# A gated attention mixer at the end of a transformer kernel: second-branch products beside the last heads, gating by pairs, key scores released unit by unit

## The chip, the cores and the metric

The kernel is one program on one core of a Trainium2 chip. The metric is the time of one execution on the device in microseconds (us); the profile adds a span (first to last instruction) and the times of each engine: PE is TensorE, DVE is VectorE, ACT is ScalarE, POOL is GpSimd, SP is the engine that only issues DMAs here.

## The reference, cut to what matters

Two residual blocks of a small model (256 tokens, width 1024) run one after the other. Each of the first block's two layers ends in an expert layer that scores keys; the second block is a mixer with two branches and then an MLP:

```python
# expert layer, twice
q = (h @ wq).reshape(B, S, PEER_HEADS, 2, half)            # 16 groups of 128
s1 = einsum('bshd,hnd->bshn', q[..., 0, :], keys[:, 0])    # key scores
s2 = einsum('bshd,hnd->bshn', q[..., 1, :], keys[:, 1])
...                                                        # top 16, gates, experts u and v

# last mixer
q, k, v, su, sv, g_a, g_b = split(h @ w_in)
y_att = sliding_window_attention(q, k, v, ...)             # 8 heads, sinks, ALiBi
y_sgu = chunked_spatial_gating(su, sv, ...)                # products over tokens, times gelu(su)
merged = sigmoid(g_a) * (y_att @ w_oa) + sigmoid(g_b) * (y_sgu @ w_ob)
x = x + merged @ w_out
x = x + conv_gated_mlp(rmsnorm(x), ...)
```

## The kernel before

All weights stream through a ring of three slots (`RING`) as pieces of 128x1024 fp32 (512 KB each). SP starts the DMA of a piece into a slot (line 312) once the low part of the piece three before it has been made. A piece is split in two fp32r parts: ACT copies it to `w_hi` (line 508), then POOL (line 404) or DVE (line 1036) subtracts to make `w_lo`. PE then takes three products for each 128 rows: high by high, high weight by low activation, low weight by high activation. A piece marked `WHOLE` is not split: PE reads the ring slot itself in fp32. Every engine has its own instruction stream in program order, and semaphores tie them together; the order inside each stream is written out by hand.

The last mixer runs so. Its projections come first: queries and keys, values, the two halves of the spatial gating, then eight gate units (`one_unit(features)`, two pieces or 48 matmuls each; PE lines 1895, 1899, 1907), which ACT copies out of three rotating banks into `s_gate` (line 588). PE runs gate unit 0, then the 16 matmuls of the spatial gating (line 2458, `sgu_mixed`), then the scores of heads 0 to 2 (line 2319), then for each head: one gate unit (the filler), the transposes of the probabilities (line 2334), the scores of head h+3, the product with the values (lines 2342 and 2343). DVE makes the normed keys (line 1628), `s_vn` for the spatial gating (line 1694), the gating's sum and product `s_yb` (lines 1698 and 1704), and per head the masked scores (lines 1638 to 1645) and the scaled probabilities (lines 1650 to 1656). ACT exponentiates (lines 809 to 811) and copies the turned probabilities out (line 823).

After head 7, ACT and DVE split both branches' outputs into high and low parts (lines 522 and 1025). The eight pieces of `sb_ab` hold w_oa above w_ob, one output chunk of 128 columns each, so PE runs 24 matmuls for each chunk (lines 2475 to 2477) and DVE merges it: a product of the bank with both sigmoids (line 1715), an addition of its two halves (line 1717). The merged activations are split again and PE starts `add_to_stream` with w_out (line 1895, 1897, 1905 for its first piece).

In an expert layer, PE runs eight query units and then waits in line 2248 until all eight are out of their banks (DVE line 1107) before the key scores (line 2255), in eight groups of four matmuls.

Of the kernel before, what the change touches and what calls it, by code (L numbers as in the profile page):

```python
# [18 lines left out]
P = 128  # L19
T = 256  # L20
# [44 lines left out]
def build(nc, a, out):  # L65

    ctx = ExitStack()
    with ctx:
# [66 lines left out]
        def b3(ap, n):  # L135
# [125 lines left out]
                ("sb_in_c", "sb_in", 24, POOL), ("sb_ab", "sb_ab", 8, POOL), ("sb_out", "sb_out", 8, POOL),  # L261
                ("up", "up", 4, (POOL, DVE)), ("up_b", "up", 2 * FC - 4, DVE), ("down", "down", FC, DVE)]
        starts, maker = {}, []
        for name, _, count, who in RUNS:
            starts[name] = len(maker)
            maker += [who[j % 2] if isinstance(who, tuple) else who for j in range(count)]
# [41 lines left out]
        def _(sp):  # L308
# [5 lines left out]
            def stream(name, array, count):  # L314
                k0, at = starts[name], 0

                def piece(j):
                    if array == "ev_in":
                        return a[array][EV_ORDER[j]]
                    if array == "ev_out":  # L320
                        half, pair = 1 - j // 4, 2 * (j % 4)
                        return a[array][pair:pair + 2, :, half * 512:(half + 1) * 512].rearrange("o p n -> p o n")
# [14 lines left out]
                loops = (count - done) // BODY if not array.startswith("ev_") else 0  # L337
# [156 lines left out]
        def _(act):  # L494
# [85 lines left out]
            def unit(outs, func=ACT.Copy, pieces=2, scale=1.0, view=None):  # L580
# [4 lines left out]
                src = unit_bank(u[0])[:, 0:pieces * T]  # L585
# [218 lines left out]
            def attention(p, filler):  # L804
# [10 lines left out]
                for h in range(p["heads"]):  # L815
# [8 lines left out]
                    if h % 2:  # L824
                        act.wait_ge(g["at_mixed"], c + 1)
                        A(p["y"][:, h // 2, :], bank[7][:, 0:T], ACT.Copy).then_inc(g["at_y"], 1)

# [88 lines left out]
            act.wait_ge(g["units_out"], u[0])  # L916
            for c in range(KC):
                v = s_gate.rearrange("p (b c t) -> p b c t", b=2, c=KC)[:, :, c, :]
                A(v, v, ACT.Sigmoid).then_inc(g["gate_open"], 1)
# [87 lines left out]
        def _(dve):  # L1007
# [622 lines left out]
            def attention(p):  # L1630
                for h in range(p["heads"] + 1):
                    if h < p["heads"]:
# [12 lines left out]
                        V.tensor_scalar(sm[:, 0:2], sm[:, 0:2], nsink[:, h:h + 1], None, ALU.min).then_inc(g["at_masked"], 1)  # L1645
                    if h >= 1:
# [9 lines left out]
                        V.tensor_scalar(PR[:, P:3 * P], PR[:, P:3 * P], sm[:, 7:8], None, ALU.mult).then_inc(g["at_prob"], 1)  # L1656

# [38 lines left out]
            dve.wait_ge(g["sgu_mixed"], 1)  # L1696
            for j in range(2):
                step(V.tensor_tensor(s_mix[:, j * 512:(j + 1) * 512].rearrange("p (c b t) -> p c b t", c=2, b=TB),
                                     bank[6 + j][:, :].rearrange("p (c b t) -> p c b t", c=2, b=TB),
                                     s_bs[:, j * 256:(j + 1) * 256].rearrange("p (c o t) -> p c o t", c=2, o=1).to_broadcast([P, 2, TB, P]),  # L1700
                                     ALU.add))
            settle()
            dve.wait_ge(g["units_out"], u[0] + 8)
            V.tensor_tensor(s_yb, s_mix, s_u, ALU.mult).then_inc(g["sgu_y"], 1)
            attention(swa_att)
            u[0] += 16
            lows_of(big[:, at_y:at_y + 8 * T])
            dve.wait_ge(g["units_out"], u[0])
            n[0] += 31
            gates = s_gate.rearrange("p (b c t) -> p b c t", b=2, c=KC)  # L1710
            for c in range(KC):
                dve.wait_ge(g["pieces_used"], n[0] + c + 1)
                dve.wait_ge(g["gate_open"], c + 1)
# [885 lines left out]
```

## Time and profile before

| | us |
|---|---|
| median of 3 runs | 2280.3 (2279.82 to 2280.7) |
| profiled execution | 2284.43 |
| its span | 2281.5 |
| PE busy | 2234.4 (98%) |
| DVE busy | 1568.1 (69%) |
| ACT busy | 1189.8 (52%) |
| POOL busy | 774.2 (34%) |
| mean granted TensorE clock | 0.995 |

A busy PE is not a PE at its peak, since matmuls overlap. What the table says is that PE stands still for some 47 us out of 2281, in many places. The last mixer lies between about 1925 and 2081 us from the start of the span, the key scores at 202 and 1153 us.

### The profile page before, as it was taken

How to read it: one execution, taken by the hardware profiler on the slowest of the kernel's cores; microseconds unless marked ns; L12 is line 12 of the kernel's file. 1: busy time of each engine (PE TensorE's matmuls, PEld its weight loads, DVE VectorE, ACT ScalarE, POOL GpSimd, SP SyncE). 2: the span in 40 equal slices, each digit the busy share in tenths (PEclk: the TensorE clock that was granted, in tenths of full speed). 3: DMA queues.
4: the chain of work that ended last, by engine and by line, in shares of the span. 5: the costliest groups of instructions: out<-in, count | busy, mean ns of one | idle time of the engine just before them, and what ended most of it. 6: DMA issues, size and time to landing. Idle time of an engine off the chain costs nothing.

```text
span 2281.5 us, 43893 instructions
## 1 busy us (share of the span) xinstructions
PE 2234.4 (98%) x14296; PEld 1939.1 (85%) x14296; DVE 1568.1 (69%) x3187; ACT 1189.8 (52%) x1888; POOL 774.2 (34%) x766
## 2 busy tenths in 40 slices
PE   8999999999999999998999999999999999999999
PEld 7889888888888888897988888888888888888877
DVE  6733885888888755545258768888886555535885
ACT  4145555555444455565455565554444556556764
POOL 0027888222332000033778862223320002664000
PEclk9999999999999999998999999999999999999999
DMA  5345655555555566552555655555556655444655
GB/s 159 102 128 157 188 190 175 178 173 170 172 174 173 177 193 194 181 183 88 163 157 188 186 183 167 173 165 176 174 175 185 193 193 176 135 135 152 189 175 165
DMA packets 109649, 385.62 MB, mean 169 GB/s; under 512 B 12512, under 2 KB 14848, under 8 KB 109312
## 3 DMA queue, kind: packets, MB, share of 16 engines
q1 hardware_dynamic: 106864, 382.34, 53.7%
q10 hardware_dynamic: 2704, 2.23, 0.3%
q8 instruction: 47, 0.77, 0.1%
q14 instruction: 34, 0.28, 0.0%
HBM read 383.46 MB, written 1.06 MB: 169 GB/s over the span
## 4 chain that ended last, share of the span: by engine, by line
PE 93%; DVE 3%; ACT 1%; DMA 1%; issue 1%; POOL 1%; SPq 0%; DVEq 0%; ACTq 0%; POOLq 0%
PE bank L1998 23%; PE bank L1978 12%; PE bank L2048 11%; PE bank L2050 11%; PE bank L2049 11%; PE bank L1895 3%; PE bank L1907 3%; PE bank L1899 3%; PE bank L2104 3%; PE bank L2287 3%; PE bank L2230 1%; PE bank L2255 1%; PE bank L2098 1%; PE bank L2153 1%; DVE x_parts L1077 1%
## 5 line engine op out<-in xcount | busy, mean ns | idle before, releaser
L508 ACT ACTIVATE w_hi<-ring 128x1024 fp32r<-128x1024 f32 x689 | 727.8, 1057 | 544.6 <-PE bank L2050 403.4
L404 POOL TENSOR_TENSOR w_lo<-ring,w_hi 128x1024 fp32r<-128x1024 f32 x226 | 544.4, 2415 | 800.1 <-ACT w_hi L508 784.7
L1036 DVE TENSOR_TENSOR w_lo<-ring,w_hi 128x1024 fp32r<-128x1024 f32 x463 | 567.9, 1227 | 235.2 <-ACT w_hi L508 229.6
L1998 PE MATMUL bank<-x_parts,w_hi 128*128 128x512 f32 x2320 | 586.2, 394 | 0.2 <-ACT w_hi L508 0.2
L1998 PEld LDWEIGHTS bank<-x_parts,w_hi 128*128 128x128 f32 x2320 | 416.6, 189 | 74.8 <-issue 0.4
L2048 PE MATMUL bank<-w_hi,x_parts 128*128 128x512 f32 x1112 | 439.3, 395 | 0.9 <-DVE x_parts L1043 0.9
L2050 PE MATMUL bank<-w_lo,x_parts 128*128 128x512 f32 x1112 | 433.6, 390 | 0.0
L2049 PE MATMUL bank<-w_hi,x_parts 128*128 128x512 f32 x1112 | 432.5, 389 | 0.0
L1978 PEld LDWEIGHTS bank<-x_parts,w_lo 128*128 128x128 f32 x2368 | 324.8, 190 | 25.0 <-DVE w_lo L1036 2.9
L416 POOL COPY quads<-sco 128x32 f16 (+1 forms) x256 | 169.8, 691 | 514.2 <-DVE sco L1494 514.1
L1978 PE MATMUL bank<-x_parts,w_lo 128*128 128x256 f32 x2368 | 336.7, 282 | 0.2 <-DVE w_lo L1036 0.2
L2050 PEld LDWEIGHTS bank<-w_lo,x_parts 128*128 128x128 f32 x1112 | 208.7, 188 | 44.5
L2048 PEld LDWEIGHTS bank<-w_hi,x_parts 128*128 128x128 f32 x1112 | 208.9, 188 | 43.2 <-DVE w_lo L1036 0.9
L2049 PEld LDWEIGHTS bank<-w_hi,x_parts 128*128 128x128 f32 x1112 | 209.1, 188 | 41.9
L1895 PE MATMUL bank<-x_parts,w_hi 128*128 128x256 f32 x720 | 181.3, 289 | 9.3 <-ACT x_parts L533 7.9
L1899 PE MATMUL bank<-x_parts,w_hi 128*128 128x256 f32 x656 | 160.8, 283 | 0.0
L1895 PEld LDWEIGHTS bank<-x_parts,w_hi 128*128 128x128 f32 x720 | 138.6, 192 | 15.4 <-issue 8.8
L734 ACT ACTIVATE sco<-bank 128x256 f32<-128x256 f32 x136 | 52.2, 384 | 183.8 <-PE bank L1978 183.8
L1486 DVE TENSOR_TENSOR sco<-iota,quads 128x512 f16<-128x512 f16 (+1 forms) x256 | 130.3, 551 | 7.1 <-POOL quads L416 7.1
L1899 PEld LDWEIGHTS bank<-x_parts,w_hi 128*128 128x128 f32 x656 | 125.8, 192 | 0.1
L1043 DVE TENSOR_TENSOR x_parts<-big,x_parts 128x256 fp32r<-128x256 f32 x278 | 116.2, 418 | 0.0
L734 ACT ACTIVATE big<-bank 128x256 f32<-128x256 f32 x120 | 45.9, 384 | 130.9 <-PE bank L1978 130.8
(299 smaller groups left out, 2511.9 us busy)
## 6 DMA issues: line engine op xcount, KB each, us to landing
ring<-u_dram SPq DMA_DIRECT2D x256, 512.0 KB, 3.5
ring<-v_dram SPq DMA_DIRECT2D x256, 512.0 KB, 3.5
ring<-up_dram SPq DMA_DIRECT2D x44, 512.0 KB, 3.6
ring<-wq_dram SPq DMA_DIRECT2D x32, 512.0 KB, 3.6
ring<-sb_in_dram SPq DMA_DIRECT2D x31, 512.0 KB, 3.6
ring<-od_in_dram SPq DMA_DIRECT2D x25, 512.0 KB, 3.6
ring<-down_dram SPq DMA_DIRECT2D x22, 512.0 KB, 3.6
ring<-ev_in_dram SPq DMA_DIRECT2D x21, 512.0 KB, 3.6
```

Source lines behind the costliest of these rows:

```text
L404: pool.tensor_tensor(w_lo[:, k % RING, :], ring[:, k % RING, :], w_hi[:, k % RING, :].bitcast(F32), ALU.subtract).then_inc(g["lo_pool"], 1)
L416: last = pool.tensor_copy(dst[:, at + r], v.to_broadcast([P, GROUP_T, QUAD]))
L508: A(w_hi[:, k % RING, :], ring[:, k % RING, :], ACT.Copy).then_inc(g["w_hi_done"], 1)
L1036: V.tensor_tensor(w_lo[:, k % RING, :], ring[:, k % RING, :], w_hi[:, k % RING, :].bitcast(F32), ALU.subtract).then_inc(g["lo_dve"], 1)
L1486: return V.tensor_tensor(fours(dst), keys.to_broadcast(shape), of_token[:, row].to_broadcast(shape), ALU.is_equal)
L1895: mm(dst, hi[:, rows[c]], xh[:, c, :], start=(c == 0), stop=False)
L1899: mm(dst, hi[:, rows[c]], xl[:, c, :], start=False, stop=False)
L1978: return mm(dst[:, 0:T], lo[:, rows[c]], xh[:, c, :], start=False, stop=False, skip_group_check=True)
L1998: mm(dst[:, :], hi[:, rows[c]], x_both[:, c, :], start=(c == 0), stop=False, skip_group_check=True)
L2048: mm(dst, xh[:, s, t], hi[:, cols], start=False, stop=False, skip_group_check=True)
L2049: mm(dst, xl[:, s, t], hi[:, cols], start=False, stop=False, skip_group_check=True)
L2050: last = mm(dst, xh[:, s, t], lo[:, cols], start=False, stop=False, skip_group_check=True)
```

## The change

Five edits, in three places.

1. Two gate units run ahead of the heads in place of one, and heads 0 to 5 have a gate unit each. The spatial gating's matmuls move behind the scores of heads 0 to 2 on PE; on DVE its sum and product move behind the mask of head 1.
2. The eight pieces of `sb_ab` are cut the other way: four pieces with w_ob's rows for two output chunks each, then four with w_oa's. The first is `WHOLE`. The w_ob pieces run as `sgu_unit` 0 to 2 beside heads 5, 6 and 7, and `sgu_unit` 3 behind head 7; their results go through the rotating banks and ACT into `s_m`.
3. The splits of both branches' outputs are single steps between the heads: `y_high` on ACT, `y_low` on DVE.
4. The merge goes by pairs of chunks: the w_ob part in `s_m` is multiplied by its gate in place, the bank of the w_oa part by its gate, and the two are added. The sigmoids are taken over 512 adjacent columns.
5. In both expert layers the wait for all query units becomes a wait for two units ahead of each of the first four groups of key scores.

```diff
-                ("sb_in_c", "sb_in", 24, POOL), ("sb_ab", "sb_ab", 8, POOL), ("sb_out", "sb_out", 8, POOL),
+                ("sb_in_c", "sb_in", 24, POOL), ("sb_ab", "sb_ab", 8, (WHOLE,) + 7 * (POOL,)), ("sb_out", "sb_out", 8, POOL),
...
+                    if array == "sb_ab":
+                        half, pair = 1 - j // 4, 2 * (j % 4)
+                        return a[array][pair:pair + 2, :, half * 512:(half + 1) * 512].rearrange("o p n -> p o n")
...
             gate_unit(0)
-            attention(swa_att, lambda h: gate_unit(h + 1) if h < 7 else None)
-            act.wait_ge(g["at_y"], 4)
-            act.wait_ge(g["sgu_y"], 1)
-            split(big[:, at_y:at_y + 8 * T], lambda j: None)
+            gate_unit(1)
...
+            def beside(h):
+                if h < 6:
+                    gate_unit(h + 2)
+                if h == 5:
+                    y_high(2, "sgu_y", 1)
+                    y_high(3, "sgu_y", 1)
...
+            def behind(h):
+                if h >= 5:
+                    sgu_unit(h - 5)
+                if h == 6:
+                    y_high(0, "at_y", 2)
+                if h == 7:
+                    y_high(1, "at_y", 4)
...
+            for j in range(4):
+                for at in (2048, 0):
+                    v = s_gate[:, at + j * 512:at + (j + 1) * 512]
+                    A(v, v, ACT.Sigmoid).then_inc(g["gate_open"], 1)
+                if j == 0:
+                    sgu_unit(3)
                 n[0] += 1
                 highs(n[0] + 2)
-            split(s_m, lambda j: act.wait_ge(g["merged"], 2 * j + 2))
+            split(s_m, lambda j: act.wait_ge(g["merged"], j + 1))
...
+            def behind(h):
+                if h == 7:
+                    y_low(2, 1)
+                    y_low(3, 2)
+                if h == 8:
+                    y_low(0, 3)
+                    y_low(1, 4)
+
+            attention(swa_att, lambda h: sgu() if h == 1 else None, behind)
...
+                step(V.tensor_tensor(v, v, s_gate[:, 2048 + j * 512:2048 + (j + 1) * 512], ALU.mult))
+                dve.wait_ge(g["pieces_used"], n[0] + j + 1)
+                dve.wait_ge(g["gate_open"], 2 * j + 2)
+                V.tensor_tensor(pr, (bank[6], bank[7], bank[3], unit_bank(u[0] + 20))[j][:, :], s_gate[:, j * 512:(j + 1) * 512], ALU.mult).then_inc(g["merged_out"], 1)
+                settle()
+                dve.wait_ge(g["merged_out"], j + 1)
+                V.tensor_tensor(v, v, pr, ALU.add).then_inc(g["merged"], 1)
...
                 raw_units(1 + 2 * layer, layer == 1, 8)
-                pe.wait_ge(g["units_out"], u[0])
                 pe.wait_ge(g["keys_loaded"], 16 * (layer + 1))
                 for s in range(8):
                     if s >= 4:
                         pe.wait_ge(g["scores_out"], 8 * layer + s - 3)
+                    else:
+                        pe.wait_ge(g["units_out"], u[0] - 6 + 2 * s)
...
+            attention(swa_att, lambda h: one_unit(features) if h < 6 else None, lambda h: sgu_unit(h - 5) if h >= 5 else None)
+            sgu_unit(3)
+            pe.wait_ge(g["x_lo_done"], splits + 4)
+            for j in range(4):
+                if j == 3:
+                    pe.wait_ge(g["units_out"], u[0] - UNITS + 1)
+                two_chunks((bank[6], bank[7], bank[3], unit_bank(u[0]))[j], 0)
             add_to_stream()
```

## Rows read from the trace of the kernel before

**Rows 1.** The page: the chain that ended last by engine, and its costliest group.

```profile
PE 93%; DVE 3%; ACT 1%; DMA 1%; issue 1%; POOL 1%; SPq 0%; DVEq 0%; ACTq 0%; POOLq 0%
...
L508 ACT ACTIVATE w_hi<-ring 128x1024 fp32r<-128x1024 f32 x689 | 727.8, 1057 | 544.6 <-PE bank L2050 403.4
```

**Rows 2.** Waits of PE, 1960 to 2062: total us, times, longest.

```profile
PE bank L2458 <- DVE big L1694: 4.2, 1, 4.2
PE bank L2342 <- ACT big L823: 2.8, 4, 0.7
PE bank L2475 <- DVE x_parts L1025: 2.0, 1, 2.0
```

**Rows 3.** Timeline of PE: start, us, engine, line, tiles, count, idle before.

```profile
1967.38 3.36 PE L2458 MATMUL bank<-big 128*64 128x128 f32 x32 [4.18 <-DVE big L1694]
1970.67 1.57 PE L2319 MATMUL bank<-big 64*128 64x128 f32 x12
```

**Rows 4.** Stretches: length, busy time by engine, then granted clock, DMA share, GB/s.

```profile
1967.38:1970.80 3.42, 3.42 (x34) 3.25 (x36) 0.02 (x1) 0.00 (x0) 0.00 (x0) 0.58 0.31 125
...
2032.20:2035.20 3.00, 2.95 (x14) 2.98 (x15) 1.71 (x3) 2.97 (x5) 0.00 (x0) 0.52 0.03 5
```

**Rows 5.** Timeline of DVE in the last mixer.

```profile
1960.11 2.48 DVE L1628 SCALAR_TENSOR_TENSOR big<-big,qk_gain 128x512 f32<-128x512 f32 x1 [10.86 <-ACT big L578]
...
1965.92 1.40 DVE L1694 SCALAR_TENSOR_TENSOR big<-big 128x512 f32<-128x512 f32 x2
...
1972.11 1.22 DVE L1704 TENSOR_TENSOR big<-big 128x1024 f32<-128x1024 f32 x1
...
1978.72 2.07 DVE L1654 TENSOR_SCALAR big<-big 128x128 f32<-128x128 f32 x1
1980.82 2.40 DVE L1656 TENSOR_SCALAR big<-big 128x256 f32<-128x256 f32 x1
...
2036.70 0.69 DVE L1715 TENSOR_TENSOR big<-bank,big 128x512 f32<-128x512 f32 x1 [2.80 <-PE bank L2477]
2037.43 1.19 DVE L1717 TENSOR_TENSOR big<-big 128x256 f32<-128x256 f32 x1
...
2057.53 0.42 DVE L1717 TENSOR_TENSOR big<-big 128x256 f32<-128x256 f32 x1
2057.87 2.49 DVE L1025 TENSOR_TENSOR x_parts<-big,x_parts 128x512 fp32r<-128x512 f32 x4
```

**Rows 6.** Timeline of POOL in the last mixer.

```profile
1959.63 2.40 POOL L404 TENSOR_TENSOR w_lo<-ring,w_hi 128x1024 fp32r<-128x1024 f32 x1 [2.24 <-ACT w_hi L508]
1962.56 2.90 POOL L404 TENSOR_TENSOR w_lo<-ring,w_hi 128x1024 fp32r<-128x1024 f32 x1 [0.52 <-ACT w_hi L508]
1978.31 7.18 POOL L404 TENSOR_TENSOR w_lo<-ring,w_hi 128x1024 fp32r<-128x1024 f32 x3 [12.86 <-ACT w_hi L508]
...
2035.92 7.53 POOL L404 TENSOR_TENSOR w_lo<-ring,w_hi 128x1024 fp32r<-128x1024 f32 x3 [8.18 <-ACT w_hi L508]
...
2060.03 2.60 POOL L404 TENSOR_TENSOR w_lo<-ring,w_hi 128x1024 fp32r<-128x1024 f32 x1 [2.51 <-ACT w_hi L508]
```

**Rows 7.** Timeline of PE behind the products with w_oa and w_ob.

```profile
2057.58 0.36 PE L1895 MATMUL bank<-x_parts,w_hi 128*128 128x256 f32 x1 [0.81 <-POOL w_lo L404]
...
2059.64 1.28 PE L1905 MATMUL bank<-x_parts,w_hi 128*128 128x256 f32 x8
```

**Rows 8.** Timelines of PE: a piece taken whole, and one low part of a split piece.

```profile
105.31 3.72 PE L2104 MATMUL bank<-big,ring 128*128 128x256 f32 x16
...
1962.08 1.12 PE L1907 MATMUL bank<-x_parts,w_lo 128*128 128x256 f32 x8
```

**Rows 9.** Key scores: waits of PE over the span, PE's and DVE's timelines.

```profile
PE bank L2255 <- DVE big L1107: 2.8, 2, 1.4
...
1153.26 7.41 PE L2255 MATMUL bank<-big 128*128 128x128 f32 x64 [1.40 <-DVE big L1107]
...
1152.52 0.69 DVE L1107 TENSOR_TENSOR big<-bank,big 128x512 f32<-128x512 f32 x1
```

**Rows 10.** Timeline of ACT at the first heads.

```profile
1977.19 1.99 ACT L508 ACTIVATE w_hi<-ring 128x1024 fp32r<-128x1024 f32 x2
```

More of the change, by code:

```diff
@@ L336, in stream @@
                     done += 1
-                loops = (count - done) // BODY if not array.startswith("ev_") else 0
+                loops = (count - done) // BODY if array != "sb_ab" and not array.startswith("ev_") else 0
                 if loops:
@@ L578, in roots, with unit @@
                     A(dst, dst, ACT.Exp, scale=-0.5).then_inc(g[done], 1)
-            def unit(outs, func=ACT.Copy, pieces=2, scale=1.0, view=None):
+            def unit(outs, func=ACT.Copy, pieces=2, scale=1.0, view=None, whole_bank=False):
                 n[0] += pieces
@@ L1702, in _ @@
[L1702 to L1713, printed above, removed]
-                pr = s_prod[:, (c % 2) * 512:(c % 2 + 1) * 512]
-                V.tensor_tensor(b3(pr, 2), b3(bank[c % 4][:, :], 2), gates[:, :, c, :], ALU.mult).then_inc(g["merged_out"], 1)
-                dve.wait_ge(g["merged_out"], c + 1)
-                V.tensor_tensor(s_m[:, c * T:(c + 1) * T], pr[:, 0:T], pr[:, T:2 * T], ALU.add).then_inc(g["merged"], 1)
@@ L1718, in _, with sgu @@
-            n[0] += 8
+            def sgu():
+                dve.wait_ge(g["sgu_mixed"], 1)
+                for j in range(2):
+                    step(V.tensor_tensor(s_mix[:, j * 512:(j + 1) * 512].rearrange("p (c b t) -> p c b t", c=2, b=TB),
+                                         bank[6 + j][:, :].rearrange("p (c b t) -> p c b t", c=2, b=TB),
+                                         s_bs[:, j * 256:(j + 1) * 256].rearrange("p (c o t) -> p c o t", c=2, o=1).to_broadcast([P, 2, TB, P]),
+                                         ALU.add))
+                settle()
+                dve.wait_ge(g["units_out"], u[0] + 8)
+                V.tensor_tensor(s_yb, s_mix, s_u, ALU.mult).then_inc(g["sgu_y"], 1)
@@ L2451, in _ @@
             one_unit(features)
-            pe.wait_ge(g["sgu_v_ready"], 2)
-            pe.wait_ge(g["sgu_w_ready"], 1)
+            one_unit(features)
             pe.wait_ge(g["sb_qk_ready"], 3)
-            for gr in range(SG):
-                for b in range(TB):
-                    c = gr // 2
-                    last = mm(bank[6 + c // 2][64 * (gr % 2):64 * (gr % 2) + 64, ((c % 2) * TB + b) * P:((c % 2) * TB + b + 1) * P],
-                              s_vn[:, b * 512 + gr * SGD:b * 512 + (gr + 1) * SGD], s_ws[:, gr * P:(gr + 1) * P],
-                              start=True, stop=True)
@@ new lines, in _, with two_chunks @@
+            splits = 4 * xs[0]
+            next_split()
+            def two_chunks(dst, half):
+                hi, lo, low_ready = weights_in_turn(0, 0)
+                low_ready()
+                for m in range(2):
+                    for k in range(4):
+                        to, rows, c = dst[:, m * T:(m + 1) * T], slice(m * 512 + k * P, m * 512 + (k + 1) * P), 4 * half + k
+                        mm(to, hi[:, rows], xh[:, c, :], start=(m == k == 0), stop=False, skip_group_check=True)
+                        mm(to, hi[:, rows], xl[:, c, :], start=False, stop=False, skip_group_check=True)
+                        last = mm(to, lo[:, rows], xh[:, c, :], start=False, stop=False, skip_group_check=True)
@@ L2478, in _, with sgu_unit @@
                 last.then_inc(g["pieces_used"], 1)
                 n[0] += 1
+            def sgu_unit(q):
+                pe.wait_ge(g["units_out"], u[0] - UNITS + 1)
+                if q:
+                    pe.wait_ge(g["x_lo_done"], splits + 2)
+                    two_chunks(unit_bank(u[0]), 1)
+                else:
+                    pe.wait_ge(g["sgu_y"], 1)
+                    pe.wait_ge(slot_loaded[n[0] % RING], 16 * (n[0] // RING + 1))
+                    w = ring[:, n[0] % RING, :]
+                    for m in range(2):
+                        for k in range(4):
+                            last = mm(unit_bank(u[0])[:, m * T:(m + 1) * T], w[:, m * 512 + k * P:m * 512 + (k + 1) * P],
+                                      s_yb[:, k * T:(k + 1) * T], start=(m == k == 0), stop=False, skip_group_check=True)
+                    last.then_inc(g["pieces_used"], 1)
+                    n[0] += 1
+                u[0] += 1
```

75 lines of the change are left out of this document (43 added, 32 removed).

## The prediction, on record before the change was built

> **What bounds the kernel now.** I read the chain of work that ended last first: 93% of the span is PE's [rows 1]. So an edit is worth what it takes off PE's line: a wait of PE, a slower clock, or PE work itself. Everything on ACT, DVE and POOL counts only where PE waits for it. Next came the waits of PE in the last mixer, which are what edits 1 to 4 can remove: 4.2 us ahead of the spatial gating's matmuls for `s_vn`, four waits of 0.7 us for the copy of the turned probabilities (heads 0, 5, 6 and 7), and 2.0 us ahead of the products with w_oa and w_ob for the low parts [rows 2]. Third, the granted clock: it is 0.58 of full in the stretch behind the 4.2 us gap and 0.52 in the stretch behind the last heads, that is mostly the lower of the two levels (1.2 against 2.4 GHz), and PE had done little just before both [rows 4]. Then, since the change moves DVE's and POOL's work against each other, their timelines side by side [rows 5, 6].
>
> Those two timelines hold the reading on which the forecast turns. A DVE step that reads and writes SBUF alone stops for as long as POOL is inside one of its subtractions. The line 1628 step that begins at 1960.11 lasts 2.48 us with a subtraction at 1959.63, line 1654 takes 2.07 and line 1656 2.40 us under the three from 1978.31; line 1717 takes 1.19 us at 2037.43 under those from 2035.92, and 0.42 us at 2057.53 with POOL idle. The step of line 1715, which reads a bank, takes 0.69 us under the same subtractions. POOL waits likewise: its subtraction at 1962.56 lasts 2.90 us and not 2.40 [rows 5, 6]. From these starts and ends I take that POOL holds the two for about 2.26 us and a 512-column DVE step for 0.55, and that they alternate when both are waiting: 2.81 us for each pair.
>
> The Trainium skill says the same, GPSIMD Engine Reference, section 1, Specifications: GpSimd's way into SBUF is shared with VectorE, with contention for instructions that have two SBUF inputs or run in a 2-port mode. The trace agrees (1.19 against 0.42 us for line 1717). It speaks against this change, whose merge has two such steps for each pair of chunks; without it the sum below would come out as the first rival's.
>
> **What the change takes from PE's line.** The 4.18 us gap ahead of line 2458 goes, because gate unit 1 fills it [rows 3]. Without the gap the clock should not fall, so the gating's matmuls need 3.36 x 0.58 = 1.95 us: 1.4 saved [rows 3, 4]. The four 0.7 us waits go or are covered by other products: 2.8. The 1.95 us wait for the low parts goes in its old form, and 3.0 us at 0.52 become 1.6: 1.4 more [rows 2, 4]. Together 4.2 + 1.4 + 2.8 + 2.0 + 1.4 = 11.8 us. Moving gate units and w_ob pieces costs nothing in itself; PE runs them somewhere.
>
> **What it adds, in order.** (a) The whole piece. A split piece is 24 matmuls of 0.12 us ((1.12 - 0.28)/7 between starts): 2.88. A whole one is 16 passes, 3.72 us with the tail of 0.16: 3.56 [rows 8]. +0.7.
>
> (b) `s_vn`. With gate unit 1 behind gate unit 0, ACT makes the next two high parts at once and POOL goes on from 1965.4 without the idle time that it has now (12.86 us before 1978.31). The two line 1694 steps, 1.40 us together now [rows 5], meet two more subtractions: the last line 1628 step ends at 1966.0, the first `s_vn` at 1968.8, the second at 1971.7. PE is through gate unit 1 and three scores at 1970.3, so it waits 1.4 us. Bounds 0 and 1.8.
>
> (c) Head 0's probabilities. DVE now does mask 0, mask 1, the gating's sum (1.3) and `s_yb` (1.22 [rows 5]), and only then the scaling; that runs from about 1971.8 to 1977.3. ACT is through with the exponentials of head 1 by 1975.6 and makes the next high part (1.06 us [rows 1, 10]), so POOL starts near 1976.7, 0.6 us ahead of the scaling. Its two steps then take what lines 1654 and 1656 take in [rows 5] at 1978.72, some 4.5 us in all. They end near 1981.9; PE has finished gate unit 2 at 1979.4: 2.5 us of waiting. Bounds 0 and 3.
>
> (d) End of the heads. On ACT the high part of the next w_oa piece (1 us) and the copy of `sgu_unit` 2 stand in front of `y_high` of the last heads, so POOL is inside a subtraction when `y_low` comes: its 0.6 us become 1.9. PE waits 1.5 us for it, then 0.9 for the low part of the second w_oa piece, whose high part is queued behind the table load and two sigmoids; 0.4 more is scattered over heads 6 and 7. 2.8; bounds 1 and 3.5.
>
> So far 0.7 + 1.4 + 2.5 + 2.8 = 7.4: the products with w_oa end 4.4 us earlier than now, at 2052.2 against 2056.6.
>
> (e) The merge, where most of that goes back. Now DVE has one SBUF step (256 columns) per chunk, the last 0.42 us [rows 5]; then it will have two of 512 per pair. The first bank is ready at 2043. POOL is then making the low parts of the last w_oa piece and of the w_out pieces one behind the other. Four DVE steps (addition 0, multiplication 1, addition 1, multiplication 2) alternate with four subtractions: 4 x 2.81 = 11.2 us. Then POOL is done and five steps of 0.6 to 0.73 follow: 3.3. With the bank step at its head the last addition ends at 2043 + 0.6 + 11.2 + 3.3 = 2058.1; now it ends at 2057.95. From there to w_out's second piece now takes 2.8 us (2060.76, the end of the row at 2059.64 less its tail [rows 7]). It will take about 2.5, or 4.8 if the last low part falls behind POOL's next subtraction. Now DVE is ahead in that race by 0.35 us (the fourth of the steps from 2057.87 starts at 2059.68, POOL at 2060.03 [rows 5, 6]); with ACT no longer behind in its high parts I find them within 0.05 us, an even chance. So the second w_out piece begins 0.5 us earlier or 1.8 later; I take the mean, 0.7 later.
>
> (f) The clock in that hole. Between 2052.2 and 2058.6 PE has only half a piece's high products, about 1 us, as little as ahead of the two falls in [rows 4]. One fall costs 1.4 us. I take 1.2; bounds 0 and 2.8.
>
> Edits 1 to 4: +1.9 us, from -0.5 to +4.7. Their DMAs are the same eight of 512 KB at the same ring distance; the whole piece keeps its slot until PE has read it, which POOL's subtraction no longer needs, and the piece behind it in that slot is used three pieces later: nothing.
>
> (g) Key scores. PE waits 1.4 us in each layer for the eighth unit, whose step starts at 1152.52 and takes 0.69 [rows 9]. Eight groups take 7.2 us, so the fourth, which alone needs that unit, comes 2.7 us after the first: the whole 1.4 is covered. Next late could be the first expert piece; its low part is made from 1154.05 and PE gets to it at 1159. ACT's copies (0.6 against 0.9 us per group) keep up. -2.8 for both layers; bounds -3.1 and -1.4.
>
> **Sum.** +1.9 - 2.8 = -0.9 us: a span of 2280.6 for 2281.5 and a profiled execution of 2283.5 for 2284.43. The median of the runs is 4.1 below the profiled execution, and I carry the difference over: 2279.4.
>
> **Rivals.** *First: POOL is out of the way.* The waits in (b) to (e) hang on orders of 0.5 us. For it: the steps exist in the old kernel mostly uncovered (1.40 us for line 1694). Against it: rows 5 and 6 show the stop each time that both engines are busy. Walking the streams with no such stop puts w_out's second piece near 2051.5, 9.2 us earlier, and the time at 2268.3. Half of the stops gone gives about 2273.8; that is this rival's time.
>
> *Second, and slower: the clock.* The new form has four places where PE does little for 1.3 to 4 us: before the gating, before head 0's transposes, before w_oa, and in the merge. If each takes the lower level (1.4 us each) and the last low part loses its race, the sum is +1.9 + 4.2 + 1.1 - 2.8 = +4.4, or 2284.7, and 2285 to 2286 with a second stretch in the merge. One fall beyond mine already makes it slower than before (2280.8). Against it: the other gaps are shorter than the 4.18 us one, and 0.7 us ones did nothing.
>
> *Third: the key scores give nothing*, because the covered wait turns up at the first expert piece or the DVE work behind it. 2282.2. Against it: 1154.05 is early.
>
> **How the numbers follow.** Forecast 0.58, first rival 0.22, second 0.10, third 0.10. About 0.2%, 4.6 us, is what a measurement here can tell from no change: below 2275.7 is faster, above 2284.9 slower. Faster: 0.22 and a tail of the forecast, 0.25. Slower: part of the second rival, 0.07. Within: 0.68. The range takes in half of the first rival and the bounds of (d) to (g): 2272.5 to 2283.5.
>
> **What would show it.** Right: no wait at line 2255 before the first group; waits of PE of 1 to 3 us at the gating's matmuls and at line 2334 of head 0; multiplications and additions of the merge that last 2 to 3 us with POOL inside line 404; a hole in PE of 2 to 4 us in w_out's first piece. Wrong: merge steps of 0.7 us throughout (first rival), or more than two stretches at the lower clock in the mixer (second). The prediction fails most easily in the orders of half a microsecond in (c) and (e).

## The result and the profile after

The changed kernel takes 2287.3 us (median of 20 runs, 2284.2 to 2290.9) against 2281.35 for the kernel before beside it: a ratio of 1.0024, 95% interval 1.0018 to 1.0031. That is 4 to 7 us slower, and 5.5 by the ratio. The forecast was 2279.4, with 2283.5 as the upper end. The profiled execution took 2285.54, with a span of 2283.8.

The spans alone mislead. The profiled execution of before happened to run 10.2 us in an earlier stage (from 1045.2) at the lower clock, and that of after did not. So from here on I measure the last mixer by itself, from PE's first matmul of gate unit 0 to the first matmul of the next norm's sum. PE's timeline, before and then after (start, us, engine, line, tiles, count):

```profile
1957.19 0.38 PE L1895 MATMUL bank<-x_parts,w_hi 128*128 128x256 f32 x1
...
2087.39 1.03 PE L1826 MATMUL bank<-big,one 128*128 128x256 f32 x4
```

```profile
1950.33 0.38 PE L1945 MATMUL bank<-x_parts,w_hi 128*128 128x256 f32 x1
...
2089.34 1.02 PE L1876 MATMUL bank<-big,one 128*128 128x256 f32 x4
```

The mixer took 2087.4 - 1957.2 = 130.2 us before and 139.0 after: edits 1 to 4 cost 8.8 us. Edit 5 gives about 3 back (below), which leaves the 5.5 of the ratio.

Waits of PE in the changed kernel from 1930 to 2070 (total us, times, longest); they stand in the place of [rows 2]:

```profile
PE bank L2386 <- DVE big L1687: 4.9, 2, 2.7
PE bank L1945 <- ACT x_parts L525: 4.4, 3, 2.5
PE bank L2529 <- DVE x_parts L1743: 1.4, 1, 1.4
PE bank L2514 <- DVE big L1726: 1.3, 1, 1.3
PE bank L2529 <- POOL w_lo L407: 0.8, 1, 0.8
```

The 4.2, the four 0.7 and the 2.0 of [rows 2] are gone, as the change means them to be. But 12.8 us of waits stand there where 9.8 stood (with the 0.8 of [rows 7]). PE's timeline gives each its place: ahead of the gating, the whole piece in passing, head 0's transposes, head 7's transposes, the first and second w_oa piece, and three times in w_out's first piece:

```profile
1964.93 2.02 PE L2514 MATMUL bank<-big 128*64 128x128 f32 x32 [1.33 <-DVE big L1726]
...
2018.19 3.62 PE L2547 MATMUL bank<-big,ring 128*128 128x256 f32 x16
...
1975.18 0.78 PE L2386 MATMUL bank<-ident,big 128*128 128x128 f32 x3 [2.29 <-DVE big L1687]
...
2029.46 0.55 PE L2386 MATMUL bank<-ident,big 128*128 128x128 f32 x3 [2.65 <-DVE big L1687]
...
2039.59 0.39 PE L2529 MATMUL bank<-x_parts,w_hi 128*128 128x256 f32 x1 [1.37 <-DVE x_parts L1743]
2043.56 0.36 PE L2529 MATMUL bank<-x_parts,w_hi 128*128 128x256 f32 x1 [0.84 <-POOL w_lo L407]
...
2053.23 0.36 PE L1945 MATMUL bank<-x_parts,w_hi 128*128 128x256 f32 x1 [0.81 <-ACT x_parts L525]
...
2056.88 0.39 PE L1945 MATMUL bank<-x_parts,w_hi 128*128 128x256 f32 x1 [2.46 <-ACT x_parts L525]
...
2058.88 0.58 PE L1945 MATMUL bank<-x_parts,w_hi 128*128 128x256 f32 x1 [1.08 <-ACT x_parts L525]
```

The second loss is the clock. Three stretches of the changed kernel's mixer ran at half the full clock, the lower of the two levels (length, busy time by engine with counts, granted clock, DMA share, GB/s):

```profile
1975.38:1982.21 6.83, 6.83 (x26) 5.12 (x25) 6.25 (x16) 2.61 (x7) 2.36 (x1) 0.50 0.25 79
2030.00:2033.41 3.41, 3.41 (x19) 3.41 (x18) 0.00 (x1) 0.49 (x1) 0.00 (x0) 0.50 0.49 159
2057.30:2064.10 6.80, 5.72 (x27) 5.42 (x26) 3.16 (x6) 2.64 (x3) 4.01 (x2) 0.50 0.08 10
```

Each begins within 0.6 us of the end of a wait of 2.3 to 2.7 us. That is 17.1 us at half clock where the kernel before has 6.8 (the two of [rows 4]).

The rows of the merge. DVE's and then POOL's timeline:

```profile
2042.75 0.69 DVE L1763 TENSOR_TENSOR big<-bank,big 128x512 f32<-128x512 f32 x1 [2.48 <-PE bank L2531]
2043.55 2.78 DVE L1766 TENSOR_TENSOR big<-big 128x512 f32<-128x512 f32 x1
2046.25 2.90 DVE L1760 TENSOR_TENSOR big<-big 128x512 f32<-128x512 f32 x1
2049.08 0.68 DVE L1763 TENSOR_TENSOR big<-bank,big 128x512 f32<-128x512 f32 x1
...
2051.90 2.86 DVE L1760 TENSOR_TENSOR big<-big 128x512 f32<-128x512 f32 x1
...
2057.47 0.69 DVE L1766 TENSOR_TENSOR big<-big 128x512 f32<-128x512 f32 x1
...
2041.02 13.19 POOL L407 TENSOR_TENSOR w_lo<-ring,w_hi 128x1024 fp32r<-128x1024 f32 x5 [2.04 <-ACT w_hi L511]
```

The steps that read SBUF alone take 2.1 to 2.9 us while POOL is inside its five subtractions and 0.69 behind them; the step that reads a bank takes 0.68 us either way.

### The profile page after: what moved, and what is told of

It reads as the page before. It is cut to its first block, busy times and chain, and to the rows that moved or that the text cites. A ratio compares the mean times of both kernels' runs of the same rounds, so it can differ in the third digit from the quotient of the medians.

```text
span 2283.8 us, 43879 instructions
## 1 busy us (share of the span) xinstructions
PE 2235.0 (98%) x14288; PEld 1937.7 (85%) x14288; DVE 1581.5 (69%) x3183; ACT 1189.6 (52%) x1891; POOL 772.7 (34%) x765
## 4 chain that ended last, share of the span: by engine, by line
PE 92%; DVE 4%; ACT 1%; issue 1%; DMA 1%; POOL 0%; SPq 0%; DVEq 0%; ACTq 0%; POOLq 0%
PE bank L2048 23%; PE bank L2028 12%; PE bank L2098 11%; PE bank L2100 11%; PE bank L2099 11%; PE bank L1945 3%; PE bank L1949 3%; PE bank L1957 3%; PE bank L2154 3%; PE bank L2338 3%; PE bank L2280 1%; PE bank L2306 1%; PE bank L2148 1%; PE bank L2203 1%; DVE x_parts L1107 1%
## 5 line engine op out<-in xcount | busy, mean ns | idle before, releaser
L737 ACT ACTIVATE big<-bank 128x256 f32<-128x256 f32 x120 | 45.9, 384 | 130.5 <-PE bank L2028 130.5
```

## The experiments

My theory after seeing the result: the port that DVE and POOL share makes the new waits of PE, and the lower clock behind those waits is what the forecast left out. Rivals: the order of the work alone makes the waits and POOL only coincides with them; and the clock stretches belong to one execution, not to the kernel. "The mixer" below is the stretch defined above, taken from each kernel's own profiled execution.

| kernel | median us | ratio to before | mixer us | of it at the lower clock |
|---|---|---|---|---|
| before | 2281.35 | 1 | 130.2 | 6.8 |
| changed | 2287.29 | 1.0024 | 139.0 | 17.1 |
| `e1_keys` | 2279.15 | 0.9986 (0.9977 to 0.9994) | 131.0 | 10.2 |
| `e2_mixer` | 2288.99 | 1.0031 (1.0022 to 1.0041) | 134.3 | 6.8 |
| `e3_warm` | 2280.59 | 0.9996 (0.9987 to 1.0005) | 132.7 | 0 |
| `e4_padd` | 2282.82 | 1.0005 (0.9996 to 1.0014) | 135.4 | 10.2 |
| `e6_old_warm` | 2276.42 | 0.9974 (0.9965 to 0.9984) | 128.0 | 0 |
| `e7_first` | 2281.13 | 0.9996 (0.9987 to 1.0004) | 129.8 | 6.8 |
| `e8_short_new` | 2268.16 | 0.9939 (0.9925 to 0.9953) | 119.7 | 0 |
| `e9_short_old` | 2276.65 | 0.9971 (0.9963 to 0.9980) | 123.5 | 0 |
| `e5_both` | 2281.93 | 1.0000 (0.9991 to 1.0009) | 132.0 | 0 |
| `e10_warm_merge` | 2287.05 | 1.0017 (1.0006 to 1.0028) | 137.2 | 10.2 |
| `e11_warm_heads` | 2282.27 | 1.0003 (0.9994 to 1.0012) | 133.4 | 3.4 |
| `e12_first_warm` | 2274.42 | 0.9971 (0.9960 to 0.9981) | 127.4 | 0 |

Differences between two kernels are taken from their ratios below, at 22.8 us for 0.01.

**Edit 5 alone, and edits 1 to 4 alone.** `e1_keys` is the kernel before with the new wait ahead of the key scores:

```diff
-                pe.wait_ge(g["units_out"], u[0])
                 for s in range(8):
                     if s >= 4:
...
+                    else:
+                        pe.wait_ge(g["units_out"], u[0] - 6 + 2 * s)
```

> The kernel before with edit 5 alone (a wait for two units ahead of each of the first four groups of key scores). Theory (port and clock): the changed kernel gained here and lost in the mixer. In its trace the first key scores come 1.5 us earlier in each layer, so 2.9 us less than before, about 2278.4 us for 2281.35. Rival (the gain is given back behind the scores, at the first expert piece or in DVE's ranking): no difference, and then the mixer cost only 5.9 us.

Measured: 3.2 us faster than before (1.4 to 5.2 by the interval). The forecast had 2.8.

`e2_mixer` is the changed kernel with that one diff undone.

> The changed kernel with the old wait ahead of the key scores, so edits 1 to 4 alone. Theory (port and clock): 8.8 us more than before, about 2290 us (5.9 measured for the whole change and 2.9 that the key scores give). Rival (key scores give nothing): 5.9 us more, 2287.3.

Measured: 7.1 us slower than before (5.0 to 9.4). The two parts add up to what the whole shows (7.1 - 3.2 = 3.9; the whole: 5.5, 4.1 to 7.1), so the loss lies in the mixer and edit 5 is a gain.

**PE kept busy in its waits.** `e3_warm` is the changed kernel with dummy matmuls (256 columns into a bank that is free) ahead of the waits, so that the waits stay but PE isn't idle in them. The pair (25, 12) stands for the groups ahead of the fifth and the seventh pair of products in w_out's first piece:

```diff
                 for h in range(3):
                     score(h)
+                keep_warm(12, 7)
                 sgu()
...
                     if h == 0:
+                        pe.wait_ge(g["sgu_y"], 1)
+                        keep_warm(20, 7)
+                    if h == 7:
+                        pe.wait_ge(g["at_pt"], c)
+                        keep_warm(20, 6)
...
             sgu_unit(3)
+            keep_warm(12, 6)
...
-            add_to_stream()
+            add_to_stream((25, 12))
```

> The changed kernel with dummy matmuls (bf16, 256 columns, into a bank that is free) where PE waits: 12 ahead of the spatial gating's, 20 ahead of the transposes of head 0 and of head 7, 12 ahead of the w_oa products, 25 and 12 in w_out's first piece. The sources are the same, and the output is. Theory (the clock is most of the miss): the changed kernel's trace has 17.1 us at the lower level in the mixer, five stretches of 3.4 us at some 1.4 us each; with PE kept at work they go, and the time falls by 5 to 7 us, to about 2281. Rival (it is the waits alone, the clock costs what it cost before): no gain, or up to 2 us lost, since the dummies that overrun the wait lie on PE's line.

Measured: 0.0028 below the changed kernel, 6.4 us; the mixer is 132.7 us, 6.3 less, with no stretch at the lower clock. The work is otherwise the same, so the clock cost 6.3 us at least; where dummy matmuls outlast a wait they take some of the gain back.

`e6_old_warm` does the same for the kernel before with edit 5 (32 dummy matmuls ahead of the 4.2 us gap, 14 ahead of the 2.0 us one).

> The kernel before with the new key wait (edit 5) and with PE kept busy by dummy matmuls of 256 columns in the two gaps of its last mixer, 32 of them ahead of the spatial gating and 14 ahead of the products with w_oa and w_ob. If the clock in these gaps is what they cost beyond their length, the stretches at the lower clock behind both go and with them about 1.7 us each: 2279.2 (edit 5 alone) less 1.7 to 3.4, that is 2276 to 2277.5, and then edits 1 to 4 are worth nothing even with the clock held (the changed kernel with dummy matmuls took 2280.6). Rival: edits 1 to 4 do shorten PE's line and only the clock hid that; then this kernel stays above 2279.5, at best level with edit 5 alone, and the changed order with the clock held is the better one of the two relative to its own start.

Measured: 0.0012 below `e1_keys`, 2.7 us; the mixer is 128.0 us, 2.2 less than before. The first reading held: with the clock held in both, the changed order is still 0.0022, 5.0 us, behind the old one (132.7 against 128.0 in the mixer). The clock takes 6.3 us in the new order and 2.2 in the old, 4.1 of the 8.8.

**Where the clock costs.** `e11_warm_heads` has only the first four of the dummy groups, `e10_warm_merge` only the last two.

> The changed kernel with dummy matmuls only ahead of the gating, of head 0's and head 7's transposes and of the products with w_oa. The stretches of 6.8 and 3.4 us at 1975.4 and 2030.0 should go: 5.1 us at most, but the time won ahead of the merge is partly waited away in the merge's hole, whose end is set by DVE and POOL. So 2 to 4 us less than the changed kernel, 2283.5 to 2285.5. If PE's line is all that counts, 5 us less.

> The changed kernel with dummy matmuls only in w_out's first piece, that is in the merge's hole. The stretch of 6.8 us at the lower clock that begins at 2057.3 should go and no other: 3.4 us less than the changed kernel, 2283.9. If the stretches further up (head 0, head 7) are what costs, it stays at 2287.

Measured: 4.8 us less than the changed kernel with the waits ahead of the merge filled, 1.6 less with the merge's hole filled (a size inside the intervals), together the 6.4 of `e3_warm`. The merge's gain is half of what I expected. I had also thought that part of the time won ahead of the merge would be waited away in it, and it was not: the merge starts when the first bank is ready, so it moves with PE.

The mixer in two parts says where each cost lies. The first part runs from gate unit 0 to w_out's first product, the second from there to the norm (us, one profiled execution each):

| kernel | first part | at the lower clock | second part | at the lower clock |
|---|---|---|---|---|
| before | 100.4 | 6.8 | 29.8 | 0 |
| changed | 102.9 | 10.2 | 36.1 | 6.8 |
| `e3_warm` | 98.4 | 0 | 34.4 | 0 |
| `e6_old_warm` | 98.2 | 0 | 29.8 | 0 |
| `e11_warm_heads` | 98.4 | 0 | 35.1 | 3.4 |
| `e10_warm_merge` | 102.8 | 10.2 | 34.4 | 0 |
| `e2_mixer` | 98.3 | 0 | 36.0 | 6.8 |
| `e4_padd` | 102.8 | 10.2 | 32.5 | 0 |
| `e5_both` | 98.4 | 0 | 33.7 | 0 |
| `e8_short_new` | 89.6 | 0 | 30.1 | 0 |
| `e9_short_old` | 93.7 | 0 | 29.8 | 0 |

With the clock held the two orders are level up to w_out (98.4 and 98.2), and all that the new one loses it loses in the merge (34.4 against 29.8). The clock takes 4.5 us of the new order's first part, 2.2 of the old one's, and 1.7 of the new one's second.

**Does it happen each time?** In the profile of `e2_mixer`, which has the same waits, only the merge drew the lower clock, and its first part took 98.3 us, as long as `e3_warm`'s, with no dummy matmul in it. Four more executions with a profile, two of each kernel unchanged:

> The changed kernel as it is, a second profiled execution. If the lower clock follows the waits ahead of head 0, ahead of head 7 and in the merge's hole each time, 17 us of the mixer at the lower clock again; if it takes only some of them, as in the profile with the old key wait, between 7 and 17.

> The changed kernel, a third profiled execution; as the second.

> The kernel before as it is, a second profiled execution. Its 4.2 us gap and its 2.0 us one were each followed by 3.4 us at the lower clock, 6.8 in all; with edit 5 they were followed by 10.2. Each time between 3.4 and 10.2 us, below the changed kernel's.

> The kernel before, a third profiled execution; as the second.

Stretches of the changed kernel's third execution:

```profile
1976.10:1982.93 6.83, 6.75 (x24) 5.04 (x25) 6.25 (x17) 2.53 (x7) 2.36 (x1) 0.50 0.33 96
2030.70:2034.10 3.40, 3.40 (x19) 3.40 (x18) 0.25 (x1) 0.49 (x1) 0.00 (x0) 0.50 0.43 159
2058.00:2064.80 6.80, 5.94 (x27) 5.65 (x28) 3.45 (x6) 2.64 (x3) 3.73 (x2) 0.50 0.02 8
```

The same three stretches at the same waits, 17.1 us, in all three executions of the changed kernel (mixer 139.0, 138.7, 138.7 us). The kernel before has 6.8 us in all three of its own, once as one stretch behind the 4.2 us gap and twice as two (130.2, 130.2, 130.5). So it is the kernels', though which wait draws it is not fixed: `e2_mixer` shows 6.8, and `e1_keys` 10.2.

**POOL's subtractions cut short.** In `e8_short_new` and `e9_short_old` POOL makes only 16 of 1024 columns of the low parts, from eight pieces ahead of the gate units (so a little earlier than the expectations say) to the last w_out piece. Most of the low parts of those weights are left out, and all else is issued as in the changed kernel and in the kernel before.

```diff
-                pool.tensor_tensor(w_lo[:, k % RING, :], ring[:, k % RING, :], w_hi[:, k % RING, :].bitcast(F32),
+                some = slice(0, 16 if starts["sb_in_c"] <= k < starts["up"] else None)
+                pool.tensor_tensor(w_lo[:, k % RING, some], ring[:, k % RING, some], w_hi[:, k % RING, some].bitcast(F32),
```

> The changed kernel with POOL's subtraction cut to 16 of 1024 columns for the pieces of the last mixer from the first gate unit on. This leaves out most of the low parts of those weights (stale values stand in their place), and PE, ACT and DVE issue the same instructions. If POOL's subtractions stop DVE's steps and this makes the new waits, the merge's steps fall from 2.1 to 2.9 us to 0.7, the waits at the gating, head 0, head 7 and in w_out's first piece shrink to under 1 us together with the lower clock behind them: 9 us of waits and 2 to 4 of clock less, 2274 to 2277. Rival: the waits come from the order in which ACT and DVE take their work, and POOL only coincides with them; then it stays within 2 us of the changed kernel's 2287.

> The kernel before with the same cut of POOL's subtractions, which leaves out the same low parts; the control for the run on the changed kernel. Its steps under POOL's subtractions lie mostly beside other work: the gap ahead of the gating shrinks by 1 to 2 us, the wait for the low parts ahead of the products by about 1, the merge not at all. 2 to 4 us faster than before, 2278 to 2280. If instead it gains as much as the changed kernel does (8 us or more), the port is not what sets the two orders apart.

Measured: 14 us below before in the new order, 6.6 in the old; the mixers are 119.7 and 123.5 us. The same steps in DVE's timeline of `e8_short_new`, three of head 0 and head 7 and three of the merge:

```profile
1972.65 0.18 DVE L1682 TENSOR_TENSOR big<-big 128x2 f32<-128x2 f32 x1
...
1973.07 0.28 DVE L1686 TENSOR_SCALAR big<-big 128x128 f32<-128x128 f32 x1
...
2023.80 0.35 DVE L1688 TENSOR_SCALAR big<-big 128x256 f32<-128x256 f32 x1
...
2035.61 0.69 DVE L1767 TENSOR_TENSOR big<-big 128x512 f32<-128x512 f32 x1
2036.32 0.69 DVE L1761 TENSOR_TENSOR big<-big 128x512 f32<-128x512 f32 x1
2037.86 0.69 DVE L1764 TENSOR_TENSOR big<-bank,big 128x512 f32<-128x512 f32 x1 [0.85 <-PE bank L2532]
```

In the changed kernel they took 2.37, 2.14 and 2.38 us (heads 0 and 7) and 2.78 and 2.90 (merge). One wait of PE above 0.5 us is left in the mixer up to w_out's second piece, 0.8 ahead of w_out, and no stretch at the lower clock. The rival "the order alone" is out: nothing in the order was changed. My expectation was too small for both kernels. In the new order all 6.3 us of the clock went, where I had 2 to 4, and 13.0 us besides, where I had 9. In the old one I had the gap ahead of the gating shrink by 1 to 2 us; it shrank from 4.2 to 0.3, and no stretch at the lower clock was left, while the 2.0 us wait for the low parts stayed. DVE's three steps ahead of that gap take 2.08 us in `e9_short_old`, and took 5.89 in the kernel before. The timelines of DVE, before and then `e9_short_old`:

```profile
1960.11 5.89 DVE L1628 SCALAR_TENSOR_TENSOR big<-big,qk_gain 128x512 f32<-128x512 f32 x3 [10.86 <-ACT big L578]
```

```profile
1960.42 2.08 DVE L1629 SCALAR_TENSOR_TENSOR big<-big,qk_gain 128x512 f32<-128x512 f32 x3 [13.52 <-ACT big L579]
```

This also splits the 8.8 us. With the clock held, POOL's full subtractions cost 132.7 - 119.7 = 13.0 us in the new order and 128.0 - 123.5 = 4.5 in the old: 8.5 more. The clock costs 4.1 more. And without either, the new order is 123.5 - 119.7 = 3.8 us better: -3.8 + 8.5 + 4.1 = 8.8. (The cut shortens POOL's own work too, so the 13.0 and the 4.5 are its cost by every path, not by the stopped DVE steps alone; PE's wait put down to POOL itself was 0.8 us in each kernel. That DVE's steps are the main path is read from their lengths above, and for the additions of the merge from the next run.)

**The merge without the second SBUF input.** `e4_padd` writes the product of each pair back to its PSUM bank, so that the addition has one input in a bank:

```diff
-                V.tensor_tensor(pr, (bank[6], bank[7], bank[3], unit_bank(u[0] + 20))[j][:, :], s_gate[:, j * 512:(j + 1) * 512], ALU.mult).then_inc(g["merged_out"], 1)
+                pr = (bank[6], bank[7], bank[3], unit_bank(u[0] + 20))[j][:, :]
+                V.tensor_tensor(pr, pr, s_gate[:, j * 512:(j + 1) * 512], ALU.mult).then_inc(g["merged_out"], 1)
```

> The changed kernel with one edit: the gate's product with the w_oa bank is written back into the bank, so that the addition of the merge has one input in PSUM and one in SBUF, not two in SBUF. Sizes and count of the steps stay. Theory (POOL's subtractions stop the SBUF-only steps): the additions of 2.78 and 2.12 us take 0.7; the merge ends 3.5 us earlier, the hole in w_out's first piece shrinks by as much, and the time falls by 3 to 5 us, to 2282.5 to 2284. Rival (the merge is late for DVE's own work or for ACT's high parts): the additions keep their length and the time stays within 1 us of 2287.3.

Timeline of DVE, and a wait of PE:

```profile
2043.06 0.69 DVE L1767 TENSOR_TENSOR big<-big,bank 128x512 f32<-128x512 f32 x1
2043.66 2.18 DVE L1760 TENSOR_TENSOR big<-big 128x512 f32<-128x512 f32 x1
...
2052.78 0.69 DVE L1767 TENSOR_TENSOR big<-big,bank 128x512 f32<-128x512 f32 x1
2053.38 4.87 DVE L1055 TENSOR_TENSOR x_parts<-big,x_parts 128x512 fp32r<-128x512 f32 x4
...
PE bank L1956 <- DVE x_parts L1055: 2.2, 1, 2.2
```

Measured: 0.0019, 4.3 us, below the changed kernel. All four additions take 0.69 us under POOL's subtractions, and the last one ends at 2053.5 instead of 2058.2. But the low parts behind them now fall under a subtraction: 4.87 us for the four and not 2.49, and PE waits 2.2 us for them. So PE's waits behind w_out's first product shrink from 3.5 us (2.46 and 1.08) to 2.2, and the stretch at the lower clock goes.

`e5_both` joins it with the dummy matmuls.

> The changed kernel with dummy matmuls in all of PE's waits of the mixer and with the merge's product written to its PSUM bank. If the merge's hole and the clock are separate costs, this takes the 6.7 us of the dummy matmuls and of the PSUM product what is left without the clock in the merge (4.5 less 3.4 for one stretch of 6.8 us): 2287.3 - 6.7 - 1.1, about 2279.5. If they are the same microseconds, 2280.6, as with the dummy matmuls alone. The old order with edit 5 and the clock held took 2276.4; if the changed order is worth anything once both its costs are gone, this kernel goes below that.

Measured: level with `e3_warm` (1.0000 against 0.9996; the mixer 0.7 us shorter). By the time of the run the two gains don't add. But the dummy matmuls in w_out's first piece were counted for the old hole, and here they outlast the new one. DVE's and PE's timelines in `e5_both`:

```profile
2052.37 4.87 DVE L1055 TENSOR_TENSOR x_parts<-big,x_parts 128x512 fp32r<-128x512 f32 x4
```

```profile
2052.77 2.90 PE L1867 MATMUL bank<-ident,zeros 128*128 128x256 bf16 x25
...
2055.99 1.49 PE L1867 MATMUL bank<-ident,zeros 128*128 128x256 bf16 x12
...
2057.79 1.12 PE L1958 MATMUL bank<-x_parts,w_hi 128*128 128x256 f32 x8
```

The low parts are there at 2057.24 and PE comes to them at 2057.79. The second part of the mixer takes 33.7 us in `e5_both` and 32.5 in `e4_padd`, which has no dummy matmuls and no lower clock there, against 34.4 in `e3_warm`. So of `e4_padd`'s 3.6 us in that part (36.1 to 32.5) some 1.7 was the clock's, and the other 1.9 can be the shorter hole. A kernel with the product in PSUM and dummy matmuls only ahead of the merge would show it; it was not run.

**Edit 1 by itself.** `e7_first` is the kernel before with gate unit 1 ahead of the scores and the gating behind them, nothing else.

```diff
             one_unit(features)
+            one_unit(features)
...
                 for h in range(3):
                     score(h)
+                sgu()
```

> The kernel before with edit 1 alone (gate unit 1 ahead of the scores, the gating behind them). By the prediction's steps it takes away 4.2 us of gap, 1.4 of clock and one wait of 0.7, and adds 1.4 ahead of the gating and 2.5 ahead of head 0's transposes: 2.4 us faster than before, 2280.0. If the lower clock follows the new waits ahead of head 0, as in the changed kernel (6.8 us of it, 3.4 us lost), it is 1 us slower than before instead, 2283.4. Rival: edit 1 is where all of the loss comes from, and w_ob's products and the merge cost nothing; then this kernel is 5 to 9 us slower than before.

PE's timeline at the gating and at head 0:

```profile
1970.03 2.02 PE L2465 MATMUL bank<-big 128*64 128x128 f32 x32 [1.26 <-DVE big L1696]
1980.26 0.55 PE L2338 MATMUL bank<-ident,big 128*128 128x128 f32 x3 [2.29 <-DVE big L1658]
```

Measured: 0.9 us faster than before, its interval from 3.0 faster to 0.9 slower; between the forecast's 2.4 and the 1 us slower with two stretches at the lower clock. Its two waits are those of the changed kernel to within 0.1 us, so (b) and (c) belong to edit 1, and head 7's 2.65 us and the merge's hole to edits 2 to 4, which carry all of the loss that can be told from the noise.

`e12_first_warm` adds edit 5 and dummy matmuls ahead of the gating, head 0 and the products.

> The old merge with edit 1, edit 5 and dummy matmuls ahead of the gating, of head 0's transposes and of the products with w_oa and w_ob. Against the same without edit 1 (2276.4) it says what edit 1 is worth with the clock held: the gap of 4.2 us goes, waits of 1.3 and 2.3 us come, and one wait of 0.7 ahead of head 0 goes too. 0.6 to 1.3 us less, 2275.1 to 2275.8. Rival: edit 1 turns ACT's and DVE's order against the later heads too (waits of 1.4 us for turned probabilities stood in its trace where there were 0.7), and nothing is left: 2276 to 2277.5.

Measured: 2274.4 us, 0.0029 below before, 6.6 us (4.3 to 9.1). It is faster than both kernels. Edit 1's own share in it can't be told by the ratio (0.0003, 0.7 us, below `e6_old_warm`, inside the intervals); the mixer, 127.4 against 128.0 us, says the same size.

## Why the prediction was wrong

| step | forecast us | measured us |
|---|---|---|
| old waits removed | 4.2 + 2.8 + 2.0 | gone |
| (a) whole piece | 3.72 | 3.62 |
| (b) ahead of the gating | 1.4 | 1.33 |
| (c) head 0 | 2.5 | 2.29 |
| (d) first and second w_oa piece | 1.5, 0.9 | 1.37, 0.84 |
| (d) heads 6 and 7 | 0.4 | 2.65 |
| (e) from first bank to last addition | 15.1 | 2058.16 - 2042.75 = 15.4 |
| (e) last low part against POOL | even chance, +1.1 | DVE 2059.88, POOL 2059.85; POOL waited, 0 |
| clock in the mixer, against before | -2.8 + 1.2 | +4.1 |
| edits 1 to 4 up to w_out's first product | -4.4 | +2.5 |
| edits 1 to 4 behind it | +6.3 | +6.3 |
| edits 1 to 4 | +1.9 | +8.8 |
| (g) keys | -2.8 | -3.2 |

**Right.** The port reading held. Steps (b), (c), both halves of (d) at w_oa, and the merge up to its last addition came within 0.3 us. In the changed kernel PE waits nowhere at the key scores, where before it waited 1.4 us twice. The extreme of the first rival, no stops at all, was put 12.0 us below before; the run with POOL cut short was 13.9 below, which is near, though it leaves out POOL's own time too. DVE's scaling at head 0, with POOL's two subtractions beside it:

```profile
1969.99 2.37 DVE L1681 TENSOR_TENSOR big<-big 128x2 f32<-128x2 f32 x1
...
1972.59 2.14 DVE L1685 TENSOR_SCALAR big<-big 128x128 f32<-128x128 f32 x1
...
1969.86 4.79 POOL L407 TENSOR_TENSOR w_lo<-ring,w_hi 128x1024 fp32r<-128x1024 f32 x2 [5.53 <-ACT w_hi L511]
```

The order was one I had not seen (the tiny 128x2 step is the one that is caught, 0.13 us behind POOL's start), but the price is the one forecast. That is luck in part: two steps were stopped, as I had it, but the 128x2 product and the 128x128 scaling, and not the two scalings. The Trainium skill, SBUF — State Buffer, section Who interferes with whom, says that a VectorE instruction with two SBUF inputs, or in a 2-port mode, is blocked until a GpSimd one that reads SBUF and started first is through, and that one with at most one SBUF input outside those modes doesn't contend; the trace agrees with both (2.78 us for the addition from SBUF, 0.69 in `e4_padd` with one input in a bank, both under POOL's subtractions).

**Wrong, first: the clock, about 5.7 us of the 6.9 missed.** Step (f) allowed the lower clock in one place, the merge, at 1.2, and took the old kernel's two stretches off. But (b), (c) and (d) put waits of 1.3 to 2.5 us into PE's line, and the trace of before already had such a case: the stretch behind the 2.0 us wait, at 0.52 [rows 2, 4]. I used this row to claim the gain of 1.4 us when that wait goes, and not to price the new waits of the same length. The second rival had this mechanism, with 0.10 for it and 2284.7 to 2286 as its time; "the other gaps are shorter than the 4.18 us one" was the wrong comparison, since the 2.0 us one stood in the same group. Three stretches came, of 6.8, 3.4 and 6.8 us: two of them twice as long as those I priced at 1.4 each.

**Wrong, second: head 7, 2.3 us.** I had 0.4 us scattered over heads 6 and 7. PE waited 2.65 ahead of head 7's transposes, for the scaling of its probabilities. DVE's and POOL's timelines there:

```profile
2027.02 2.38 DVE L1687 TENSOR_SCALAR big<-big 128x256 f32<-128x256 f32 x1
...
2024.05 2.40 POOL L407 TENSOR_TENSOR w_lo<-ring,w_hi 128x1024 fp32r<-128x1024 f32 x1 [5.29 <-ACT w_hi L511]
2026.91 2.34 POOL L407 TENSOR_TENSOR w_lo<-ring,w_hi 128x1024 fp32r<-128x1024 f32 x1 [0.46 <-ACT w_hi L511]
```

DVE came 0.11 us after POOL's start. The mechanism was in the text, its place wasn't; the prediction named such orders as what it would fail by, for (c) and (e), but not for (d).

**Sum.** The clock 5.7 and head 7 2.3 make 8.0; (a) to (d) otherwise came 0.6 us shorter than forecast and the merge without its clock 0.5 shorter (34.4 - 29.8 = 4.6 for 5.1). That leaves the 6.9 between +1.9 and +8.8. By place, the whole miss lies ahead of w_out: from gate unit 0 to w_out's first product the changed kernel takes 2.5 us more than before (2053.23 - 1950.33 against 2057.58 - 1957.19, [rows 7]), where I had 4.4 less, and from there on 6.3 more, which is what I had (4.4 + 1.9). That last agreement is luck in part: I had 1.2 of clock and 5.1 of waits there, and 1.7 and 4.6 came. Also, the end of (e) doesn't follow from its own numbers: 2058.1 + 2.5 is 0.2 us before 2060.76, and 2058.1 + 4.8 is 2.1 behind it, so the mean is 1.0 later and not 0.7, and the forecast should have been 0.3 higher.

**Open.** Which of several waits of 1 to 3 us is followed by the lower clock in a given execution: the same wait ahead of head 0 drew 6.8 us of it in the changed kernel, 3.4 in `e7_first` and none in `e2_mixer`. The 2.0 us wait of the kernel before drew 3.4 us in two of its three executions and none in the third. Moving ACT's and DVE's work so that head 7's scaling misses POOL's subtraction was not tried.

## What to carry to other kernels

A wait of PE that a change creates should be priced with its clock, by the shortest wait in the old trace that is followed by a lower granted clock; here four waits of 1.3 to 2.7 us and those at w_out and in the merge (12.8 us in all) cost another half of their length, though not each of them drew it. Where POOL subtracts the low parts of the weights, a DVE step from SBUF costs not its own 0.15 to 0.7 us but up to a whole subtraction, so packing more of them (or a longer chain ahead of PE's next product) under a dense run of POOL's work loses what the denser order wins. Reading one operand from PSUM freed the addition, and dummy matmuls in a wait that can't be removed gave the clock's part back; they have to be counted anew when the wait shrinks, since what outlasts it stands in PE's line.

## What the runs showed of the chip that I had not expected

- A 128x2 product of 0.15 to 0.18 us was stopped for 2.37 us behind a subtraction that began 0.13 us earlier, and in the same kernel a step with one SBUF tensor and two columns took 2.31 us where it takes 0.23 at 1976.26, with no subtraction beside it. So steps of 2 to 512 columns were all stopped for up to a whole subtraction. The row of the second, and POOL's beside it:

```profile
1978.80 2.31 DVE L1675 TENSOR_SCALAR big<-big,gate_s 128x2 f32<-128x2 f32 x1
...
1978.72 2.36 POOL L407 TENSOR_TENSOR w_lo<-ring,w_hi 128x1024 fp32r<-128x1024 f32 x1 [4.08 <-ACT w_hi L511]
```

- Waits of PE of 2.3 to 2.7 us were followed by 3.4 to 6.8 us at the lower clock, in three executions out of three of the changed kernel; in the one of `e2_mixer`, with the same waits, only the one in the merge was. A mixer of 139 us lost 6.3 us to it.
- 101 dummy matmuls (14389 matmuls for 14288), which compute nothing, made the changed kernel 6.4 us faster.
